# Block norms of a two-block transformer kernel: the last token tile handled by column halves, one scaling moved behind the epsilon addition, and two multiplications of the double norm moved to GpSimd

## What is computed

```python
def rmsnorm(x, w):
    xf = x.astype(jnp.float32)
    y = xf * lax.rsqrt(jnp.mean(xf * xf, axis=-1, keepdims=True) + EPS)
    return (y * w.astype(jnp.float32)).astype(x.dtype)
```

## Time and profile before

| | |
|---|---|
| median of three runs | 1620.81 us |
| the profiled execution | 1619.69 us |
| its span | 1618.1 us |
| TensorE busy | 1550.6 us, 96% |
| VectorE busy | 813.6 us, 50% |
| ScalarE busy | 659.8 us, 41% |
| GpSimd busy | 223.0 us, 14% |
| mean granted TensorE clock | 0.991 |

### The profile page before, as it was taken

The page is one execution under the profiler, slowest core; times in us unless marked ns, Lnnn a source line. Parts: engine busy times, 40 slices in busy tenths (PEclk is TensorE's granted clock), DMA queues, the critical chain, the costliest instruction groups (busy, mean ns, idle before and its releaser), DMA issues. The chain is left out here.

```text
span 1618.1 us, 20712 instructions
## 1 busy us (share of the span) xinstructions
PE 1550.6 (96%) x7882; PEld 1270.7 (79%) x7882; DVE 813.6 (50%) x1634; ACT 659.8 (41%) x1369; POOL 223.0 (14%) x138
## 2 busy tenths in 40 slices
PE   7999999989899999989999999999988999999997
PEld 6888777777787889878878877777767888888886
DVE  3323288756734566546534476746566333333224
ACT  4222355565423377534225644563245322322122
POOL 0000022155300012200012233222100000000000
PEclk9999999999999999999999999989999999999999
DMA  5232211111332431123421212113220323232232
GB/s 210 91 105 91 92 60 47 52 52 43 115 96 74 143 88 51 40 79 124 148 70 65 92 66 65 41 60 97 91 66 27 104 92 104 91 98 97 94 102 78
DMA packets 39777, 137.60 MB, mean 85 GB/s; under 512 B 4928, under 2 KB 5312, under 8 KB 39552
## 3 DMA queue, kind: packets, MB, share of 16 engines
q1 hardware_dynamic: 33984, 123.75, 23.2%
q10 hardware_dynamic: 5696, 12.55, 2.6%
HBM read 128.02 MB, written 2.10 MB: 80 GB/s over the span
## 5 line engine op out<-in xcount | busy, mean ns | idle before, releaser
L213 ACT ACTIVATE cut_hi<-raw 128x1024 fp32r<-128x1024 f32 x228 | 241.7, 1060 | 605.3 <-PE ps L230 596.4
L230 PE MATMUL ps<-h_hi,cut_hi 128*128 128x512 f32 (+1 forms) x1120 | 449.8, 402 | 9.9 <-DVE arena L1233 6.2
L218 DVE TENSOR_TENSOR cut_lo<-raw,cut_hi 128x1024 fp32r<-128x1024 f32 x172 | 211.5, 1230 | 462.8 <-ACT cut_hi L213 461.0
L232 PE MATMUL ps<-h_hi,cut_lo 128*128 128x512 f32 (+1 forms) x1120 | 436.3, 390 | 0.0
L231 PE MATMUL ps<-h_lo,cut_hi 128*128 128x512 f32 (+1 forms) x1120 | 436.1, 389 | 0.0
L230 PEld LDWEIGHTS ps<-h_hi,cut_hi 128*128 128x128 f32 x1120 | 211.5, 189 | 74.5 <-issue 21.9
L232 PEld LDWEIGHTS ps<-h_hi,cut_lo 128*128 128x128 f32 x1120 | 211.2, 189 | 45.0
L231 PEld LDWEIGHTS ps<-h_lo,cut_hi 128*128 128x128 f32 x1120 | 211.6, 189 | 37.2
L218 POOL TENSOR_TENSOR cut_lo<-raw,cut_hi 128x1024 fp32r<-128x1024 f32 x56 | 134.9, 2409 | 646.7 <-ACT cut_hi L213 646.7
L230 PE MATMUL ps<-cut_hi,h_hi 128*128 128x512 f32 (+1 forms) x304 | 117.6, 387 | 7.5 <-DVE cut_lo L218 7.5
L232 PE MATMUL ps<-cut_hi,h_lo 128*128 128x512 f32 (+1 forms) x304 | 116.7, 384 | 0.0
(11 more groups left out here) (348 smaller groups left out, 2199.3 us busy)
## 6 DMA issues: line engine op xcount, KB each, us to landing
raw<-weights SPq DMA_DIRECT2D x228, 512.0 KB, 3.3
scr<-scr ACTq DMA_DIRECT2D x34, 64.0 KB, 3.6
x<-x_in SPq DMA_DIRECT2D x4, 512.0 KB, 6.5
x<-x_in ACTq DMA_DIRECT2D x1, 2048.0 KB, 7.8
q_stack<-qT_lo ACTq DMA_DIRECT2D x16, 128.0 KB, 2.3
out<-x SPq DMA_DIRECT2D x4, 512.0 KB, 2.6
consts<-tables ACTq DMA_DIRECT2D x1, 1732.0 KB, 7.8
big_row<-big_in ACTq DMA_DIRECT2D x2, 512.0 KB, 6.7
```

What stands on the lines that cost most here:

```text
L213: act.activation(cut_hi[:, u % CUT, :], raw[:, u % RAW, :], ACT.Copy).then_inc(hi_ready, 1)
L218: eng.tensor_tensor(cut_lo[:, u % CUT, :], raw[:, u % RAW, :], cut_hi[:, u % CUT, :].bitcast(F32), ALU.subtract).then_inc(lo_ready, 1)
L230: a = pe.matmul(out, left[0], right[0], start=start, stop=False)
L232: return a, pe.matmul(out, left[1], right[0], start=False, stop=stop)
```

## The change

- **Single norms behind a projection**: tile 3 is squared in two halves of 512 columns, each when its half of x is ready (`ready_half`). VectorE adds the two sums and epsilon in one 128x1 operation. The scaling of tile 2 leaves `beside` and stands behind this addition; the scaling of tile 3 is two instructions of 512 columns, and TensorE waits for the first before block 0 and for the second before block 4.
- **Double norm**: GpSimd multiplies tiles 0 and 1 by the gains, VectorE tiles 2 and 3. VectorE mixes tiles 0 and 1 beside tiles 2 and 3; the scalings of all four tiles come after the last addition to x: tiles 0, 1, then the mixing of tiles 2 and 3, then the scalings of tiles 2 and 3, the last of them by halves.

```diff
+        COLUMN_HALVES = (slice(0, 512), slice(512, 1024))
@@ class Norm
             def act(self, act):
-                for t in range(self.nt):
+                for t in range(self.nt - 1 if self.after else self.nt):
...
+                if self.after:
+                    t = self.nt - 1
+                    for half, c in enumerate(COLUMN_HALVES):
+                        act.wait_ge(*self.after.ready_half(t, half))
+                        act.activation(self.xs[:, t, c], self.src[:, t, c], ACT.Square, scale=D ** -0.5,
+                                       accum_out=ss[:, t + 45 * half:t + 45 * half + 1]).then_inc(self.squared, 1)
...
             def scale(self, dve, t):
 
                 dve.wait_ge(self.rooted, t + 1)
-                dve.tensor_scalar(self.xs[:, t, :], self.src[:, t, :], rs[:, t:t + 1], None, ALU.mult)\
-                   .then_inc(self.scaled, 1)
+                for c in COLUMN_HALVES if self.after and t == self.nt - 1 else (slice(0, D),):
+                    dve.tensor_scalar(self.xs[:, t, c], self.src[:, t, c], rs[:, t:t + 1], None, ALU.mult)\
+                       .then_inc(self.scaled, 1)
 
             def beside(self, dve, t, half):
                 if t and half == 0:
                     self.add_eps(dve, t - 1)
-                elif t:
+                elif 0 < t < self.nt - 1:
                     self.scale(dve, t - 1)
 
             def dve(self, dve):
                 if self.after:
-                    self.add_eps(dve, self.nt - 1)
-                    self.scale(dve, self.nt - 1)
+                    t = self.nt - 1
+                    dve.wait_ge(self.squared, t + 2)
+                    dve.scalar_tensor_tensor(ms[:, t:t + 1], ss[:, t:t + 1], self.eps, ss[:, t + 45:t + 46],
+                                             ALU.add, ALU.add).then_inc(self.mean, 1)
+                    self.scale(dve, t - 1)
+                    self.scale(dve, t)
...
@@ Norm.pe
                     for k in range(KD):
+                        if self.after and t == self.nt - 1 and k == KD // 2:
+                            pe.wait_ge(self.scaled, t + 2)
...
@@ class Combine, class MemoryAttention
+            def ready_half(self, t, half):
+                return self.out_dve, 2 * t + half + 1
@@ class OutA
+            def ready_half(self, t, half):
+                return self.out_dve, NT * half + t + 1
@@ class TwoNorms
             def pool(self, pool):
+                pool.wait_ge(big_loaded, 16)
+                for t in range(2):
+                    self.weigh(pool, t)
                 for t in range(NT):
                     pool.wait_ge(self.both, t + 1)
...
             def scale(self, dve, t):
 
                 dve.wait_ge(self.rooted, t + 1)
-                dve.tensor_scalar(self.xs[:, t, :], self.xs[:, t, :], rs[:, t:t + 1], None, ALU.mult)\
-                   .then_inc(self.scaled, 1)
+                for c in COLUMN_HALVES if t == NT - 1 else (slice(0, D),):
+                    dve.tensor_scalar(self.xs[:, t, c], self.xs[:, t, c], rs[:, t:t + 1], None, ALU.mult)\
+                       .then_inc(self.scaled, 1)
 
             def beside(self, dve, t, half):
                 if t == 0 and half == 0:
                     dve.wait_ge(big_loaded, 16)
-                elif half == 0:
-                    self.mix(dve, t - 1)
-                else:
+                elif t >= 2 and half == 0:
+                    self.mix(dve, t - 2)
+                elif t >= 2:
+                    dve.wait_ge(self.weighted, t)
                     self.weigh(dve, t)
-                    if t:
-                        self.scale(dve, t - 1)
 
             def dve(self, dve):
-                self.mix(dve, NT - 1)
-                self.scale(dve, NT - 1)
+                for t in range(2):
+                    self.scale(dve, t)
+                for t in range(2, NT):
+                    self.mix(dve, t)
+                for t in range(2, NT):
+                    self.scale(dve, t)
                 cut_low(dve, self.first)
```

## The result

The changed kernel had a median of 1627.02 us in 17 runs (1620.19 to 1629.86), beside 1620.91 us for the kernel before in 17 runs (1617.55 to 1627.06). The ratio is 1.0030, with a 95% interval of 1.0018 to 1.0042: slower by 0.3%, where I had given slower by over 0.2% a chance of 4% and forecast 1620.9 us. The time lies above my range.

The account below looks back on a forecast made before the run. TensorE, busy 96% of the span, was taken as the bound, waiting on VectorE at each norm. Terms -0.08 + 0.09 + 0.09 + 0.0 = +0.10 us on 1620.81 gave 1620.9 us, range 1620.5 to 1621.4.

Parts of the forecast that it names:

- The power held up by the moved scaling: Single norms: GpSimd's power takes 0.99 us instead of 0.55 while VectorE's scaling of tile 2 runs.
- the 0.07: Single norms: extra us taken for the epsilon addition, which now reads two sums.
- The single norms: Sum of three sites: norm_c -0.08 us, norm_q +0.09, norm_f +0.09.
- the 0.43: norm_q: us that moving tile 2's scaling behind the epsilon costs; possible ends 0 and 0.43.
- The double norm: Term for this site: 0.0 us, with ends -0.6 (clock full throughout) and +0.3 (start 0.28 later).
- VectorE's side: Double norm: the cut starts at 730.3 instead of 730.86, a gain of 0.5 us on VectorE.
- 16 transposes by 730.2: Double norm: TensorE's half clock ends at 730.2; 8 more at 0.108 make 731.0, where it was 730.9.
- rival 2: Double norm: TensorE at half clock longer, 1621.5 to 1623.2, say 1622.5 us; sign: clock back later than 731; chance 0.12.
- rival 3: Double norm: the clock doesn't fall, VectorE's cut limits, 0.6 us less, 1620.3 us; chance 0.1.
- GpSimd's weighings: Double norm: 2.39 us each, not stretched by VectorE's additions; rival of stretched weighings +1.4 us, 1622.3 us, chance 0.08.
- whatever the first low part gains or loses is gained or lost by the kernel: Each norm: TensorE's stream goes on at its own pace after the first low part, so its shift is the kernel's.
- a fall in the single norms: Single norms: clock also falls there, about 1.7 us each; way to over 3.2 us slower, chance 0.04.

Follow-up runs that it names:

- Filling the pause: Changed kernel plus 24 overwritten identity transposes in TensorE's double-norm pause, against the kernel before: first set median 1623.27 us; both sets mean 1622.26 +- 0.65.
- the aligned kernel: Changed kernel plus 24 dummy transposes in TensorE's double-norm pause and a 490-column VectorE write ahead of the cut: medians 1621.00 and 1620.32 us, ratios 1.0001 and 1.0000.
- weighings only: Kernel before with two double-norm weighings on GpSimd and the last tile scaled by halves, scalings of tiles 0 and 1 unmoved: median 1620.75 us, mean 1622.40 +- 1.03.
- the filled kernel before: Kernel before plus 22 overwritten identity transposes in TensorE's double-norm pause: median 1619.83 us, ratio 1.0002 (0.9988 to 1.0017).

## Why the prediction was wrong

- **The power held up by the moved scaling: right.** 0.99 instead of 0.55 in norm_c, norm_q and norm_f, 1.26 us from epsilon to scaling where I had 1.25 (without the 0.07, which was too much: the addition of two sums took 0.16). Undoing the move brought 0.55 back. The single norms sum to 0.00 where I had +0.10: in norm_q and norm_f the halves gained 0.18 and 0.16, since TensorE's transposes then limit, and the move cost 0.23 of the 0.43. The kernel with them alone is level with the one before.
- **The double norm: the mechanism was there, the size wrong.** I took 0.0, from -0.6 to +0.3, and it was +0.63 and +0.36 in two traces. VectorE's side came as worked out (cut 15.21 after the first addition; my sum had 15.0). What failed is the term "16 transposes by 730.2": I let the clock return at the same moment as before, though TensorE began later (12.1 us after the first addition, where my sum had 11.9 and the kernel before 11.6). Set against the first addition the clock came back later: at 732.75, 16.3 after it, where it had been 14.9. In the second trace it was back at 15.0; there TensorE's later start alone made the +0.36, since the 32 weight loads began 0.56 later and took 4.87 us instead of 5.06. The first trace is rival 2 in its mild form: counted from the first addition, its sign, a clock back later than 731, was passed by 0.6. Filling the pause confirmed the rest, -0.50 (I had -0.6 for rival 3). Rival 3 itself, no fall without any fill, came about in two of the 11 unfilled traces.
- **GpSimd's weighings: right**, 2.40 and 2.41. VectorE's additions beside them didn't stretch them, which agrees with the port rule that I cited from the Trainium skill (SBUF — State Buffer, SBUF: two separate sides).
- **The sum itself failed at its first premise**: "whatever the first low part gains or loses is gained or lost by the kernel". The local costs together were +0.6 us, and the median rose by 6, the mean by 4.3. From norm_c on the trace of before has some twenty pauses of TensorE of 0.8 us or more, and which of them it leaves at half clock differs from execution to execution of one and the same kernel, as the two traces of the aligned kernel show; the kernel before itself ran from 1615.65 to 1629.11 us. A write that changes nothing but times, 0.6 us in the double norm, made long times three times as frequent and cost 2.3 us in the mean. The way to a loss of over 3.2 us that I had allowed for, a fall in the single norms, is not what happened: the clock was 1.00 through all three in the changed kernel's trace. I had priced the clock at the changed sites only, and three runs within 0.2 us of each other gave no sign of such a scatter; seventeen runs of the same kernel then spread over 9.5 us. The granted clock over the whole span stood in the profile, and I looked at it around the double norm alone.
- **What stays open**: 2.0 +- 1.0 us of the changed kernel's 4.3 beyond what the delay alone gave. Either longer pauses there make for more falls than a delay of the same size, or it is scatter. Whether the delay works by the moment at which later pauses come or by the longer pause that it makes is open too. What decides at a given pause whether the clock falls was not tried; TensorE's idle time alone doesn't, since the same 1.39 us pause was followed by half clock in one trace and by full clock in the other, and so was the pause of the double norm, 3.17 us of idle weight loads.

## What to carry to other kernels

A small operation on GpSimd may be held up by a long VectorE scaling issued just ahead of it, so VectorE's idle time is not free while GpSimd works on the critical path: read how long the small operation took where the same pair already stands together. Before a sub-microsecond edit of a TensorE-bound kernel is judged by its time, look at the granted clock along the whole span, repeat both versions a dozen times, and run one version that is only delayed; the local distances in one trace were good to some hundredths where the clock was the same (4.61 to 4.63 us for the unchanged norm_q and norm_f), the whole time is not. Where TensorE had to wait for some microseconds, dummy transposes into a bank that is overwritten later kept its clock up in 7 traces of 7, though the site gains only if TensorE was what came last there, and a gain of the whole kernel wasn't shown.

## What the runs showed of the hardware that I had not expected

In the trace of before TensorE is busy throughout from 829 to 839 us (10.00 of 10.00), and yet the mean clock is 0.66, with 6.83 us at half: behind a pause of 1.83 us, that load didn't win the clock back at once. The fall came when TensorE had already been at work again for 1.3 us (the pause ended at 827.88, the half clock began at 829.16); at 678 in the changed kernel's trace it was 0.8 us (677.32 and 678.16).

Two pauses of the weight loads, 2.32 and 1.14 us with one tile turned between them (weighings only), left TensorE at half clock like one pause of 3.17 (before) or 3.73 (changed). Yet the 3.17 us were followed by full clock in two other traces.

A 0.69 us write on VectorE, in a place where it only makes TensorE wait longer, raised the mean by 2.3 +- 0.8 us. Not every edit does this: with the single norms changed 2 of 11 times were long, with the filled kernel before 1 of 12.
